# Moving four of the eight token-operand chunks to other start bytes in SBUF

## The chip, the core and the metric

The kernel runs on one NeuronCore of a Trainium2 chip. The metric is the device time of one execution in microseconds (us), the median of several runs. TensorE (PE) does the matrix products; VectorE (DVE), ScalarE (ACT) and GpSimd (POOL) do the rest; SP issues most DMAs. Every step below between two matmuls is from the start of one to the start of the next, because matmuls overlap and the duration of one is longer than the step.

## The reference

Two transformer blocks in a row on 256 tokens of width 1024. The first adds 16 meta tokens (272 rows in all), and does pooling, forgetting attention and stick-breaking attention, then a SwiGLU MLP of width 2816. The second does a gated convolution and block attention, a squared-ReLU MLP of width 4096, a linear recurrence, and a second such MLP. Cut to what carries the work:

```
proj = rmsnorm(h, norm1) @ w_in            # 1024 -> 2560 (and 6 forget logits)
h = h + concat(pool, fox, sb) @ w_out      # 1024 -> 1024
h = h + (silu(a @ w_gate) * (a @ w_up)) @ w_down          # a = rmsnorm(h, norm2), 1024 -> 2816 -> 1024
h = h + concat(conv, moba) @ ab_w_out      # from rmsnorm(h) @ ab_w_in
h = h + square(relu(rmsnorm(h) @ w_up)) @ w_down          # 1024 -> 4096 -> 1024
h = h + (rg_lru(...) * gelu(gate)) @ c_w_out
h = h + square(relu(rmsnorm(h) @ w_up)) @ w_down
out = rmsnorm(h, final_norm)
```

## The kernel before

The kernel is written out by hand for the five engines, with semaphores; every engine's order of work is the order of its code. All tokens (272 or 256 columns) stay in SBUF, with the model width on the partitions in KC = 8 chunks of 128. The weights come from HBM as 280 "slabs" of 128 x 1024 fp32, through a ring of R = 4 slots. ACT rounds each slab to fp32r (`whi`), and DVE subtracts to get the rest (`wlo`). The token operand is split in the same way into `ahi` and `alo`, so that one fp32 product is three fp32r matmuls: hi x hi, hi x lo, lo x hi. The helper `three` (L1402 to L1407) issues them.

There are two kinds of slab. A column slab (`column`, L1412) makes 128 output features: for k = 0..7 three matmuls, each with another 128 x 128 weight and with chunk k of `ahi` or `alo` as the moving operand, 24 in all. A row slab (`row`, L1462) adds to the residual: 24 matmuls that all have one moving chunk, which in the MLPs is a chunk of `hidhi` and `hidlo` (`hidden_row`, `last_rows`) and in the three output projections OUT1, OUT2 and OUT3 a chunk of `ahi` and `alo` (`operand_row`; for OUT3 chunks 0 and 1 are in `hidhi`). The MLP loops run columns and rows in turn: MLP1 has 44 columns and 22 rows, MLP2 and MLP3 32 of each; IN1, IN2 and IN3 have 20, 20 and 16 columns. After an MLP, the next stage's two first columns are issued chunk by chunk (`first_high`, `first_low`) as the operand becomes ready: ACT writes `ahi` (L563, L644, L594), DVE writes `alo` (L979, L973).

`ahi` and `alo` hold chunk k at STRIDE_A * k = 320 * k floats, which is 1280 bytes or five blocks of 256 bytes. PAD_A puts the start of both on a multiple of 256. A matmul on 256 tokens begins at token NMETA = 16, 64 bytes on; so each of the eight chunks begins at byte 64 of a block of 256. `hidhi` and `hidlo` also begin at byte 64 of a block, and each of their chunks is 1024 bytes. Matmuls on all 272 tokens (most of IN1) begin at byte 0 of a block. The weights of every matmul (`whi`, `wlo`, 512 bytes each) begin at byte 128 of a block. These places follow from the sizes of the buffers.

Of the kernel before, what the change touches and what calls it, by code (L numbers as in the profile page):

```python
# [25 lines left out]
F32 = mybir.dt.float32  # L26
F32R = mybir.dt.float32r
ALU = mybir.AluOpType
ACT = mybir.ActivationFunctionType
AX = mybir.AxisListType.X  # L30

P = 128
DM = 1024
KC = DM // P
SEQ = 256
NMETA = 16
T1 = NMETA + SEQ

STRIDE_A, PAD_A = 320, 32
EPS = 1e-6  # L40
BIG = 1.0e30

# [145 lines left out]
def build(nc, slabs, xT, par_in, fbias_in, poolw_in, gatew_in, convw_in, out):  # L188
    with ExitStack() as ctx:
        def sb(name, shape, dt=F32):  # L190
            return ctx.enter_context(nc.sbuf_tensor(name, shape, dt))
# [25 lines left out]
        whi = sb("whi", [P, R, KC, P], F32R)  # L217
        wlo = sb("wlo", [P, R, KC, P], F32R)
        h = sb("h", [P, KC, T1])
        af = sb("af", [P, KC, SEQ])  # L220

        sb("pad_a", [P, PAD_A])
        ahi = sb("ahi", [P, KC, STRIDE_A], F32R)
        alo = sb("alo", [P, KC, STRIDE_A], F32R)
        sq = sb("sq", [P, KC, T1])
        gg, half_gb = sb("gg", [P, KC]), sb("half_gb", [P, 2 * CONV_C])
        std = sb("std", [P, T1])
# [118 lines left out]
        sbs_bank = (half(gemm_bank[0], 0), half(gemm_bank[0], 1), half(aux_bank, 1))  # L346
        consts_done = 13

        def hid_buf(f, last):
            return 2 if f == last else f % 2  # L350

        def row_operand(s, k):

            if s == A_LRU and k < 2:
                return hidhi[:, k, :], hidlo[:, k, :]
            return ahi[:, k, NMETA:T1], alo[:, k, NMETA:T1]

        block = ctx.enter_context(nc.Block())

# [156 lines left out]
        def _(act):  # L516
# [40 lines left out]
            def residual_hi(i, lo=NMETA):  # L557

                for k in range(KC):
                    act.wait_ge(h_ready, KC * (i - 1) + k + 1)  # L560
                    if i < N_FINAL:
                        g = GAIN[i] + k
                        act.activation(ahi[:, k, lo:T1], h[:, k, lo:], ACT.Copy, scale=par[:, g:g + 1]).then_inc(ahi_ready, 1)  # L563
                        for j in (SQUARES_CHUNKS if i in (N_MIX0, N_MIXC) else SQUARES_ROWS).get(k, ()):
                            residual_squares(i, j)
                    else:
                        act.activation(sq[:, k, lo:], h[:, k, lo:], ACT.Square).then_inc(sq_ready, 1)  # L567
# [72 lines left out]
            for i in range(PIECES):  # L640
                act.wait_ge(x_loaded[i], 16)
                for k in (2 * i, 2 * i + 1):
                    g = GAIN[N_NORM1] + k
                    act.activation(ahi[:, k, 0:T1], h[:, k, :], ACT.Copy, scale=par[:, g:g + 1]).then_inc(ahi_ready, 1)  # L644
                for b in range(2):
                    act.wait_ge(piece_loaded[b][i], 16)
                    act.activation(whi[:, b, 2 * i:2 * i + 2, :], raw[:, b, 2 * i:2 * i + 2, :], ACT.Copy)\
                       .then_inc(hi_done if i == PIECES - 1 else piece_hi, 1)
# [294 lines left out]
        def _(dve):  # L943
# [31 lines left out]
            def residual_lo(i, s, k, lo=NMETA):  # L975

                g = GAIN[i] + k
                dve.wait_ge(ahi_ready, KC * s + k + 1)
                dve.scalar_tensor_tensor(alo[:, k, lo:T1], h[:, k, lo:], par[:, g:g + 1], ahi[:, k, lo:T1].bitcast(F32),  # L979
                                         ALU.mult, ALU.subtract).then_inc(alo_ready, 1)  # L980

            def acc_add(m, n, i, s):
# [418 lines left out]
        def _(pe):  # L1401
            def three(dst, n, j, xh, xl, start=False, stop=False):  # L1402

                hi, lo = whi[:, n % R, j, :], wlo[:, n % R, j, :]
                pe.matmul(dst, hi, xh, start=start, stop=False, skip_group_check=True)  # L1405
                pe.matmul(dst, hi, xl, start=False, stop=False, skip_group_check=True)  # L1406
                return pe.matmul(dst, lo, xh, start=False, stop=stop, skip_group_check=True)  # L1407
# [4 lines left out]
            def column(n, bank, q=0, lo=NMETA, amid=None):  # L1412

                slab_ready(n, q)
                for k in range(KC):
                    if amid and k == 3:
                        amid()
                    ins = three(bank[:, lo:T1], n, k, ahi[:, k, lo:T1], alo[:, k, lo:T1], k == 0, k == KC - 1)
                ins.then_inc(slab_used, 1)

            def first_high(n, s, k, lo=NMETA):

                pe.wait_ge(ahi_ready, KC * s + k + 1)
                for b in range(2):
                    dst, slot = gemm_bank[b][:, lo:T1], (n + b) % R
                    for w in (whi, wlo):
                        pe.matmul(dst, w[:, slot, k, :], ahi[:, k, lo:T1], start=(k == 0 and w is whi), stop=False,  # L1427
                                  skip_group_check=True)

            def first_low(n, s, k, lo=NMETA):  # L1430

                pe.wait_ge(alo_ready, KC * s + k + 1)
                for b in range(2):
                    dst, slot = gemm_bank[b][:, lo:T1], (n + b) % R
                    ins = pe.matmul(dst, whi[:, slot, k, :], alo[:, k, lo:T1], start=False, stop=(k == KC - 1),  # L1435
                                    skip_group_check=True)
                    if k == KC - 1:
                        ins.then_inc(slab_used, 1)
# [528 lines left out]
```

## Time and profile before

| | us |
|---|---|
| median of 3 runs | 877.65 (877.24, 877.65, 883.81) |
| the profiled execution | 884.41 |
| its span, first to last instruction | 882.7 |
| PE busy in it | 870.2 (99%) |
| DVE, ACT, POOL busy | 607.3, 469.2, 91.7 |
| mean granted TensorE clock | 0.998 of 2.4 GHz |

The profiled execution is 6.8 us longer than the median and 1.7 us longer than its own span. The times of the runs lie in two places, two at 877 and two (with the profiled one) at 884. Time in a part of the kernel is read from the starts of its matmuls, not from the busy time, which reads 99% at any pace.

### The profile page before, as it was taken

The page shows a single profiled execution, that of the slowest core. Times are in us where ns is not written, and L with a number is a line of the kernel's source. Part 1 is how long each engine was busy: PE and PEld are TensorE (multiplying, and loading weights), DVE is VectorE, ACT ScalarE, POOL GpSimd, SP SyncE. Part 2 cuts the span into 40 slices and gives each one's busy share as a digit, 9 for nine tenths or more (in the row PEclk, how much of TensorE's full clock was granted, in tenths as well). Part 3 has the DMA queues.
Part 4 walks back from the last instruction along what each step waited for, and adds up shares of the span by engine and source line. Part 5 has one row for each costly group of instructions (what it writes and reads, how often), then busy time and mean ns, then how long its engine had stood idle before and what let it go on. Part 6 is the DMA issues. An engine that isn't in the chain of part 4 may idle for free.

```text
span 882.7 us, 19329 instructions
## 1 busy us (share of the span) xinstructions
PE 870.2 (99%) x7298; PEld 837.3 (95%) x7298; DVE 607.3 (69%) x997; ACT 469.2 (53%) x754; POOL 91.7 (10%) x147
## 2 busy tenths in 40 slices
PE   9999999999999999999999999999999999999997
PEld 8988899999999999788999999999998999999996
DVE  5776567656656587778866666668979966666665
ACT  5646766443444485448644444445786644444443
POOL 4220001000000039520100000002110100000001
PEclk9999999999999999999999999999999999999999
DMA  7532247655565557525465555554444565555551
GB/s 254 166 120 96 97 143 250 187 183 191 173 205 173 187 161 235 163 97 178 140 212 186 185 180 182 189 191 144 171 141 168 168 212 185 181 185 187 186 171 48
DMA packets 44290, 151.61 MB, mean 172 GB/s; under 512 B 5588, under 2 KB 6868, under 8 KB 44244
## 3 DMA queue, kind: packets, MB, share of 16 engines
q1 hardware_dynamic: 41040, 145.00, 50.1%
q0 software_dynamic: 2400, 4.89, 1.7%
q10 hardware_dynamic: 804, 1.06, 0.3%
q8 instruction: 33, 0.54, 0.3%
q14 instruction: 13, 0.11, 0.0%
HBM read 148.14 MB, written 1.05 MB: 169 GB/s over the span
## 4 chain that ended last, share of the span: by engine, by line
PE 87%; DVE 6%; ACT 3%; issue 1%; DMA 1%; POOL 1%; SPq 0%; DVEq 0%; ACTq 0%; POOLq 0%
PE bank L1405 26%; PE bank L1407 26%; PE bank L1406 26%; DVE alo L979 2%; PE bank L1799 1%; DVE wlo L955 1%; PE bank L1435 1%; PE bank L1571 1%; DVE h L989 1%; PE bank L1548 1%; PE bank L1427 1%; PE bank L1889 1%; PE bank L1519 1%; DMA raw<-in_slabs 1%; ACT whi L535 1%
## 5 line engine op out<-in xcount | busy, mean ns | idle before, releaser
L1405 PE MATMUL bank<-ahi,whi 128*128 128x256 f32 (+1 forms) x1392 | 398.1, 286 | 1.0 <-DVE alo L973 0.7
L1406 PE MATMUL bank<-alo,whi 128*128 128x256 f32 (+1 forms) x1392 | 391.0, 281 | 0.0
L1407 PE MATMUL bank<-ahi,wlo 128*128 128x256 f32 (+1 forms) x1392 | 390.9, 281 | 0.0
L955 DVE TENSOR_TENSOR wlo<-raw,whi 128x1024 fp32r<-128x1024 f32 x272 | 331.0, 1225 | 26.6 <-ACT whi L535 26.6
L535 ACT ACTIVATE whi<-raw 128x1024 fp32r<-128x1024 f32 x272 | 281.2, 1050 | 92.4 <-PE bank L1407 82.7
L1405 PEld LDWEIGHTS bank<-ahi,whi 128*128 128x128 f32 x1392 | 263.0, 189 | 5.8 <-DVE alo L973 2.3
L1406 PEld LDWEIGHTS bank<-alo,whi 128*128 128x128 f32 x1392 | 264.2, 190 | 0.4
L1407 PEld LDWEIGHTS bank<-ahi,wlo 128*128 128x128 f32 x1392 | 261.5, 188 | 0.0
L1405 PE MATMUL bank<-hidhi,whi 128*128 128x256 f32 x704 | 197.8, 281 | 0.6 <-DVE wlo L955 0.6
L1406 PE MATMUL bank<-hidlo,whi 128*128 128x256 f32 x704 | 197.7, 281 | 0.0
L1407 PE MATMUL bank<-hidhi,wlo 128*128 128x256 f32 x704 | 197.7, 281 | 0.0
L1406 PEld LDWEIGHTS bank<-hidlo,whi 128*128 128x128 f32 x704 | 134.0, 190 | 0.0
L1405 PEld LDWEIGHTS bank<-hidhi,whi 128*128 128x128 f32 x704 | 133.2, 189 | 0.8 <-issue 0.8
L1407 PEld LDWEIGHTS bank<-hidhi,wlo 128*128 128x128 f32 x704 | 132.2, 188 | 0.0
L1287 DVE SCALAR_TENSOR_TENSOR y<-bank,rstd 128x256 f32<-128x256 f32 x64 | 27.1, 424 | 123.7 <-PE bank L1407 121.7
L860 ACT ACTIVATE hidhi<-y 128x256 fp32r<-128x256 f32 x64 | 26.8, 419 | 132.6 <-DVE y L1287 129.4
L403 POOL TENSOR_TENSOR sq<-sq 128x256 f32<-128x256 f32 (+1 forms) x19 | 16.2, 865 | 319.7 <-ACT sq L567 176.3
L408 POOL TENSOR_TENSOR sq<-sq 128x256 f32<-128x256 f32 x12 | 9.6, 804 | 359.4 <-ACT sq L553 181.1
L998 DVE SCALAR_TENSOR_TENSOR proj<-bank,rstd 128x256 f32<-128x256 f32 (+1 forms) x56 | 23.5, 424 | 33.0 <-PE bank L1407 30.2
L746 ACT ACTIVATE hidhi<-y 128x256 fp32r<-128x256 f32 x22 | 9.2, 418 | 59.0 <-DVE y L1171 59.0
L979 DVE SCALAR_TENSOR_TENSOR alo<-h,par,ahi 128x256 fp32r<-128x256 f32 (+1 forms) x48 | 29.2, 671 | 0.0
L1295 DVE TENSOR_TENSOR hidlo<-y,hidhi 128x256 fp32r<-128x256 f32 x64 | 27.2, 425 | 2.3
(236 smaller groups left out, 724.7 us busy)
## 6 DMA issues: line engine op xcount, KB each, us to landing
raw<-in_slabs SPq DMA_DIRECT2D x272, 512.0 KB, 3.5
shared<-in_convw POOLq DMA_DIRECT2D x4, 512.0 KB, 6.8
shared<-zpad POOLq DMA_DIRECT2D x48, 35.5 KB, 3.5
raw<-in_slabs SPq DMA_DIRECT2D x8, 128.0 KB, 5.9
vtok<-in_gatew POOLq DMA_DIRECT2D x2, 512.0 KB, 4.8
out<-y SPq DMA_DIRECT2D x4, 256.0 KB, 2.3
h<-in_xT ACTq DMA_DIRECT2D x3, 272.0 KB, 5.9
h<-in_xT SPq DMA_DIRECT2D x1, 272.0 KB, 3.3
```

What stands on the lines that cost most here:

```text
L403: pool.tensor_tensor(a, a, sq[:, 2 * j + 1, lo:], ALU.add).then_inc(sum_ready, 1)
L408: ins = pool.tensor_tensor(sq[:, a, NMETA:], sq[:, a, NMETA:], sq[:, b, NMETA:], ALU.add)
L535: act.activation(whi[:, n % R, :, :], raw[:, n % R, :, :], ACT.Copy).then_inc(hi_done, 1)
L860: act.activation(hidhi[:, hid_buf(f, FF2 - 1), :], hid[:, f % 2, :], ACT.Square).then_inc(hid_hi, 1)
L955: dve.tensor_tensor(wlo[:, n % R, :, :], raw[:, n % R, :, :], whi[:, n % R, :, :].bitcast(F32), ALU.subtract).then_inc(lo_done, 1)
L979: dve.scalar_tensor_tensor(alo[:, k, lo:T1], h[:, k, lo:], par[:, g:g + 1], ahi[:, k, lo:T1].bitcast(F32), ALU.mult, ALU.subtract).then_in ...
L998: dve.scalar_tensor_tensor(proj[:, d, lo:], src[:, lo:T1], scale, rstd[:, lo:], ALU.mult, ALU.mult).then_inc(gemm_evac, 1)
L1287: dve.scalar_tensor_tensor(hid[:, f % 2, :], col_bank(f)[:, NMETA:T1], 0.0, rstd[:, NMETA:], ALU.max, ALU.mult).then_inc(gemm_evac, 1)
L1295: dve.tensor_tensor(hidlo[:, b, :], hid2[:, f % 2, :], hidhi[:, b, :].bitcast(F32), ALU.subtract).then_inc(hid_lo, 1)
L1405: pe.matmul(dst, hi, xh, start=start, stop=False, skip_group_check=True)
L1406: pe.matmul(dst, hi, xl, start=False, stop=False, skip_group_check=True)
L1407: return pe.matmul(dst, lo, xh, start=False, stop=stop, skip_group_check=True)
```

## The change

Three of the last four chunks of `ahi` and `alo` begin later in their 1280 bytes: chunk 4 by 32 floats (128 bytes), chunk 5 by 48 (192 bytes), chunk 7 by 16 (64 bytes). With the 64 bytes of the meta tokens, chunks 4 to 7 begin at bytes 192, 0, 64 and 128 of a block of 256; chunks 0 to 3 still at 64. On all 272 tokens the starts of chunks 4 to 7 are at 128, 192, 0 and 64, those of chunks 0 to 3 at 0. Every reader and writer goes through the new helper `chunk`. The buffers have the same sizes, so nothing else moves in SBUF. No instruction is added, removed or moved, and every shape and wait stays.

```diff
+SHIFTED = {4: 32, 5: 48, 7: 16}
...
-        ahi = sb("ahi", [P, KC, STRIDE_A], F32R)
-        alo = sb("alo", [P, KC, STRIDE_A], F32R)
+        ahi = sb("ahi", [P, KC * STRIDE_A], F32R)
+        alo = sb("alo", [P, KC * STRIDE_A], F32R)
...
+        def chunk(buf, k, lo=0):
+            c = STRIDE_A * k + SHIFTED.get(k, 0)
+            return buf[:, c + lo:c + T1]
...
-            return ahi[:, k, NMETA:T1], alo[:, k, NMETA:T1]
+            return chunk(ahi, k, NMETA), chunk(alo, k, NMETA)
...
-                        act.activation(ahi[:, k, lo:T1], h[:, k, lo:], ACT.Copy, scale=par[:, g:g + 1]).then_inc(ahi_ready, 1)
+                        act.activation(chunk(ahi, k, lo), h[:, k, lo:], ACT.Copy, scale=par[:, g:g + 1]).then_inc(ahi_ready, 1)
...
-                dve.scalar_tensor_tensor(alo[:, k, lo:T1], h[:, k, lo:], par[:, g:g + 1], ahi[:, k, lo:T1].bitcast(F32),
+                dve.scalar_tensor_tensor(chunk(alo, k, lo), h[:, k, lo:], par[:, g:g + 1], chunk(ahi, k, lo).bitcast(F32),
...
-                    ins = three(bank[:, lo:T1], n, k, ahi[:, k, lo:T1], alo[:, k, lo:T1], k == 0, k == KC - 1)
+                    ins = three(bank[:, lo:T1], n, k, chunk(ahi, k, lo), chunk(alo, k, lo), k == 0, k == KC - 1)
```

`first_high`, `first_low` and the first stage's write of `ahi` are changed in the same way.

## Rows read from the trace of the kernel before

**Rows 1.** The page, parts 1 and 4: busy time, and the chain that ended last
```profile
PE 870.2 (99%) x7298; PEld 837.3 (95%) x7298; DVE 607.3 (69%) x997; ACT 469.2 (53%) x754; POOL 91.7 (10%) x147
...
PE 87%; DVE 6%; ACT 3%; issue 1%; DMA 1%; POOL 1%; SPq 0%; DVEq 0%; ACTq 0%; POOLq 0%
```
**Rows 2.** Stretches inside MLP1, MLP2, MLP3, then late in IN3: busy, count, clock
```profile
143.76:316.19 172.43, 172.43 (x1467) 172.43 (x1466) 108.74 (x149) 78.06 (x105) 0.00 (x0) 1.00 0.62 195
438.28:607.88 169.60, 169.60 (x1443) 169.60 (x1441) 106.93 (x157) 74.16 (x92) 0.00 (x0) 1.00 0.57 189
701.50:868.27 166.77, 166.77 (x1419) 166.77 (x1417) 104.37 (x153) 72.17 (x90) 0.00 (x0) 1.00 0.54 178
650.91:659.38 8.47, 8.32 (x74) 8.12 (x72) 6.42 (x13) 8.43 (x13) 0.00 (x0) 1.00 0.27 89
```
**Rows 3.** Timeline of PE in MLP1, a column and then a row
```profile
143.52 0.28 PE L1406 MATMUL bank<-alo,whi 128*128 128x256 f32 x1
143.64 0.28 PE L1407 MATMUL bank<-ahi,wlo 128*128 128x256 f32 x1
143.76 0.28 PE L1405 MATMUL bank<-hidhi,whi 128*128 128x256 f32 x1
...
144.47 0.28 PE L1405 MATMUL bank<-hidhi,whi 128*128 128x256 f32 x1
```
**Rows 4.** Timeline of PE at the end of IN3: column, then a row of OUT3
```profile
665.05 0.28 PE L1405 MATMUL bank<-ahi,whi 128*128 128x256 f32 x1
...
665.39 0.28 PE L1405 MATMUL bank<-hidhi,whi 128*128 128x256 f32 x1
...
666.07 0.28 PE L1405 MATMUL bank<-hidhi,whi 128*128 128x256 f32 x1
```
**Rows 5.** Groups of matmuls by shape over the whole span: busy us, mean ns
```profile
L1406 PE MATMUL bank<-alo,whi 128*128 128x256 f32 x1288 | 360.9, 280 | 0.0
...
L1406 PE MATMUL bank<-hidlo,whi 128*128 128x256 f32 x704 | 197.7, 281 | 0.0
```
**Rows 6.** The same view, of a stretch late in IN3
```profile
L1406 PE MATMUL bank<-alo,whi 128*128 128x256 f32 x25 | 6.9, 276 | 0.0
```
**Rows 7.** Timeline of PE: two columns of IN3 and IN2 after a stall
```profile
647.98 0.47 PE L1405 MATMUL bank<-ahi,whi 128*128 128x256 f32 x1
648.29 0.28 PE L1406 MATMUL bank<-alo,whi 128*128 128x256 f32 x1
648.41 0.28 PE L1407 MATMUL bank<-ahi,wlo 128*128 128x256 f32 x1
648.52 0.28 PE L1405 MATMUL bank<-ahi,whi 128*128 128x256 f32 x1
648.64 0.28 PE L1406 MATMUL bank<-alo,whi 128*128 128x256 f32 x1
648.75 0.28 PE L1407 MATMUL bank<-ahi,wlo 128*128 128x256 f32 x1
648.87 0.28 PE L1405 MATMUL bank<-ahi,whi 128*128 128x256 f32 x1
648.98 0.28 PE L1406 MATMUL bank<-alo,whi 128*128 128x256 f32 x1
...
335.83 0.47 PE L1405 MATMUL bank<-ahi,whi 128*128 128x256 f32 x1
336.13 0.28 PE L1406 MATMUL bank<-alo,whi 128*128 128x256 f32 x1
...
336.96 0.28 PE L1407 MATMUL bank<-ahi,wlo 128*128 128x256 f32 x1
```
**Rows 8.** Timeline of PE in IN1: 272 columns from byte 0, then 256 from byte 64
```profile
28.30 0.29 PE L1407 MATMUL bank<-ahi,wlo 128*128 128x272 f32 x1
...
29.44 0.29 PE L1407 MATMUL bank<-ahi,wlo 128*128 128x272 f32 x1
29.57 0.28 PE L1405 MATMUL bank<-ahi,whi 128*128 128x256 f32 x1
29.68 0.28 PE L1406 MATMUL bank<-alo,whi 128*128 128x256 f32 x1
...
30.25 0.28 PE L1405 MATMUL bank<-ahi,whi 128*128 128x256 f32 x1
```
**Rows 9.** Writers of the operand: timeline of DVE, then ACT's and DVE's durations
```profile
425.97 2.74 DVE L989 TENSOR_TENSOR h<-bank,h 128x256 f32<-128x256 f32 x8
...
L979 DVE SCALAR_TENSOR_TENSOR alo<-h,par,ahi x48: 471/495/1046, 8.3 to 695.6; 128x256 fp32r<-128x256 f32 x40, 128x272 fp32r<-128x272 f32 x8
...
L563 ACT ACTIVATE ahi<-h,par x40: 492/495/511, 128.9 to 693.5; 128x256 fp32r<-128x256 f32 x40
```

More of the change, by code:

```diff
@@ L643, in _ @@
                     g = GAIN[N_NORM1] + k
-                    act.activation(ahi[:, k, 0:T1], h[:, k, :], ACT.Copy, scale=par[:, g:g + 1]).then_inc(ahi_ready, 1)
+                    act.activation(chunk(ahi, k), h[:, k, :], ACT.Copy, scale=par[:, g:g + 1]).then_inc(ahi_ready, 1)
                 for b in range(2):
@@ L1426, in first_high @@
                     for w in (whi, wlo):
-                        pe.matmul(dst, w[:, slot, k, :], ahi[:, k, lo:T1], start=(k == 0 and w is whi), stop=False,
+                        pe.matmul(dst, w[:, slot, k, :], chunk(ahi, k, lo), start=(k == 0 and w is whi), stop=False,
                                   skip_group_check=True)
@@ L1434, in first_low @@
                     dst, slot = gemm_bank[b][:, lo:T1], (n + b) % R
-                    ins = pe.matmul(dst, whi[:, slot, k, :], alo[:, k, lo:T1], start=False, stop=(k == KC - 1),
+                    ins = pe.matmul(dst, whi[:, slot, k, :], chunk(alo, k, lo), start=False, stop=(k == KC - 1),
                                     skip_group_check=True)
```

## The prediction

> **What bounds the kernel now.** I read the page first: PE is busy 99% of the span, and 87% of the chain that ended last is PE [rows 1]. So the time is the number of matmuls times their step, plus the hand-overs between stages. The change touches neither the count, nor an order, nor a wait. What it can touch is the step, so I read starts, in the timeline and in the windows.
>
> In the MLPs, which hold 194 of the 280 slabs, the step is the same everywhere. In MLP1 the window of 172.43 us has 1467 matmul records, about three of them begun before it, so 1464: 117.8 ns each. MLP2 and MLP3 give the same: 169.60 us over 1440, 166.77 us over 1416 [rows 2]. The timeline shows it singly: 143.76 to 144.47 is six steps in 0.71 us, 118 ns, and it doesn't change where a column (moving operand `ahi`) hands over to a row (`hidhi`) [rows 3].
>
> The same instructions on the same addresses also run faster. At the end of IN3 the steps are 0.34 us for three and 0.68 us for six, 113.3 ns, again across the hand-over from column to row [rows 4]. The clock is 1.00 (the level of 2.4 GHz) at both places [rows 2], so it isn't the clock. There are thus **two steady paces, 117.8 and 113.3 ns**, 4.44 ns apart, and the operand's start byte (64 for all of them) doesn't alone decide between them. The duration that the page gives tells them apart too: 281 ns in the slow pace. The 704 of `hidlo` read 281 on average, so nearly all of them are slow; the 1288 of `alo` read 280.2 (360.9 us / 1288) [rows 5]. In the fast pace one reads 276 [rows 6], in a stretch of IN3 that has 74 records in 8.47 us with its stalls [rows 2]. So about 16% of the `ahi` and `alo` matmuls are fast, some 620 of 3864.
>
> What picks the pace? After a stall of PE a column can go either way. At 648.29 the steps are 120, 110, 120, 110, 120 ns in rounded figures and then 113; five steps take 0.58 us where five fast ones take 0.567, so the settling cost 13 ns. At 336.13 the seven steps to 336.96 take 0.83 us, 118.6 ns each, and it stays slow [rows 7]. Without a stall neither pace leaves its rut: MLP1 keeps one step for 172 us. The one place where the start byte changes with no stall is in IN1, from 272 columns at byte 0 to 256 at byte 64. Nine steps before it take 1.14 us (126.7 each); behind it six steps take 0.68 us, 113.3 at once [rows 8].
>
> The runs agree: 877.2 and 877.7 against 883.8 and the profiled 884.4, 6.8 us apart. One of the MLPs 2 and 3 is 64 slabs x 24 = 1536 matmuls, and 1536 x 4.44 ns = 6.8 us. I read this as one MLP that fell into the fast pace in two of the four executions. In the profiled one all three are slow.
>
> **The change, part by part.** The writers cost nothing. DVE's and ACT's instructions keep their shapes. DVE's eight adds to `h`, whose chunks are 1088 bytes apart and so begin at four different bytes of a block, take 2.74 us together, 0.34 each, with no pause; L979 and L563 have minima and medians within 24 and 3 ns of each other [rows 9], although they read those same chunks of `h`. If this cover failed, it would be 40 instructions by perhaps 24 ns, 1 us.
>
> The readers carry everything. Each column now has five changes of start byte with no stall: 64 to 192, to 0, to 64, to 128, and back to 64. That makes 164 columns x 5 = 820 changes in the kernel, where before there were hardly any. An `operand_row` of chunk 4, 5 or 7 has 24 matmuls at another byte, nine rows in all.
>
> What a change of byte does is in no row but one, the change in IN1, and there the fast pace came at once. So my step is: the slow pace depends on each matmul being like the last, a change of the start byte inside every column breaks it, and the fast pace survives. The gain if all goes fast:
> - The three MLP stretches: 1464 + 1440 + 1416 = 4320 matmuls x 4.44 ns = 19.2 us.
> - The rest of the MLPs: 194 x 24 = 4656, less 4320, is 336 x 4.44 = 1.5 us.
> - Outside the MLPs: 3864 less 108 MLP columns x 24 = 2592 leaves 1272, of which 620 are fast, so 650 x 4.44 = 2.9 us. Many of these lie behind real stalls, where the first steps are long in either pace [rows 7]; I take half, 1.4 us.
>
> Together 22.1 us. Against it stands what a change costs: from nothing (the row of IN1 [rows 8]) to a settling as behind a stall, 13 ns at 648.29 [rows 7]; with rounding up to 20. Over 820 changes that is 0 to 16 us. The nearest row is the one without a stall, so I stay near the lower end and take one change in four at 19 ns, 3.8 us. The sum: 884.41 - 22.1 + 3.8 = **866.1 us** (860.4 if a change costs nothing and the last 1.9 us come too, 878 at the dear end). The sum stands against the profiled execution, which is 6.8 us over the median; against 877.65 it is -1.3%. That the bar is the median takes away a third of the gain: part of it is had by luck already.
>
> The Trainium skill speaks against any effect. In "SBUF — State Buffer", section "Who interferes with whom", PE has a read port for the moving operand and one for the weights, independent of each other, and never waits on anyone; no page ties a matmul's speed to its start byte. By that rule the step stays what it was, and the time with it. The trace does not contradict it outright, but it shows two paces for one instruction, which the rule leaves no room for.
>
> **The rivals.**
>
> *Slower: the slow pace survives and the new bytes are dearer.* Byte 0 is the only other start that a long stretch shows: 272 columns at 126.7 ns [rows 8]. At the granted 2.4 GHz the 16 extra columns are 6.7 ns, which leaves 120.0 ns for 256, 2.2 above the slow pace; and no stretch of 272 was seen in a faster pace. If chunks 4, 5 and 7 all step so, it is 164 columns x 9 x 2.2 = 3.3 us. If in addition the fast pace is the one that doesn't survive the changes, the 620 fast matmuls lose 620 x 4.44 = 2.8 us. From the profiled execution's 884.4 that gives 887.7 to 890.5. It decides from where a change throws PE out of the fast pace more often than out of the slow one. For it: in 508 us of MLP the slow pace never broke [rows 2], though columns and rows alternate there; the fast stretches are short. Against it: the row of IN1, and the runs at 877, in which a fast MLP seems to have held for about 170 us.
>
> *Half: the fixed parts go fast, the shifted ones don't.* In a column, chunks 4 to 7 and 0 (15 matmuls) are held at about 117.8 by the changes, and 9 run at 113.3; rows run fast. 86 MLP rows x 24 x 4.44 = 9.2 us and 108 x 9 x 4.44 = 4.3 us gained, and some 26 fast columns outside lose 26 x 15 x 4.44 = 1.7 us: 884.4 - 11.8 = 872.6 us.
>
> *The change does nothing:* what picks the pace is the phase at the last stall, as now, and every run draws it per stage. Then the median stays where it was, 877.65, between 877 and 884.4. For it: both paces exist at one and the same set of addresses [rows 3, 4]. This is also what the page cited above would give.
>
> **How the numbers follow.** Forecast 0.45, of which 0.41 lies below 868.9; slower 0.26; nothing 0.17; half 0.12. A measurement of this kernel can tell about 1% from no change, so the bounds are 868.9 and 886.4 us. Faster: 0.41 and 0.01 of the half case, 0.42. Slower: 0.26 and 0.01 of the case in which nothing happens, 0.27. Within 1%: 0.31. The range runs from 858 (all fast, and a little gained at a byte that suits better than 64) to 891 (the dear end of the slower case); it leaves out about one case in ten above and one in twenty below. The likeliest case alone runs from 860 to 871. The range is wide, since the price of a change of byte rests on one row and the sign hangs on it.
>
> **What would show each step.** In the timeline inside an MLP, the step in rows (`hidhi`) should be 113.3 and the page should read 276 ns for them instead of 281. Within a column, the steps of matmuls 13 to 24 and of the next slab's first three show the price of a change; chunk 5 at 120 ns would speak for the slower case. The windows of MLP1, MLP2 and MLP3 should be about 7.0, 6.8 and 6.8 us shorter, less the changes. L979 and L563 should keep 495 ns. Repeated runs should no longer lie in two places 6.8 us apart. The prediction is wrong if rows still step at 117.8: then the start byte doesn't break the slow pace. It is wrong in size if rows step at 113.3 but columns take more than 2.76 us.

## The result and the profile after

| | before, us | after, us |
|---|---|---|
| median of 22 runs each | 883.29 (870.45 to 884.11) | 871.82 (870.92 to 873.03) |
| the profiled execution | 884.41 | 870.92 |
| its span | 882.7 | 869.2 |
| PE, DVE, ACT busy | 870.2, 607.3, 469.2 | 857.8, 607.5, 469.5 |
| mean granted clock | 0.998 | 0.999 |

The ratio is 0.9905 [0.9883, 0.9926]. It leaves out the runs of a kernel that are more than 1.5% above its fastest one, which for before means those above 883.5 us, though by their times they are of one kind with its runs at 882.7 to 883.5; the ratio of the two medians is 0.987.

More runs of before show what three could not. Over all comparisons in this study it ran 72 times: 8 times at 869.7 to 871.1 us, 31 times at 876.2 to 878.0, 33 times at 882.4 to 884.7, and never in between. The medians of the three places, 870.7, 877.0 and 883.4, are 6.3 and 6.4 us apart, about what one MLP in the fast pace is worth by the prediction (6.8 us), so I read them as two, one or none of its three MLPs in the fast pace. No trace shows before itself at 870 or 877.

How often each place comes differs between the five sets of runs that the 72 are made of: in the set above 16 of 22 lie at 882.7 to 884.1, in the set beside `only_chunk4` none of 13 (median 876.9), in the set beside `all_240` 4 of 17 (median 877.2). The sets beside the experiments ran on four different chips; whether the chip decides this is not shown. So the median of 877.65 that the prediction was given is one of the two that before shows, neither rare nor safe.

The changed kernel has one place in its 22 runs, 2.1 us wide. So the change removes a lottery. It wins 11.5 us against before's median in the same set and 13.5 us between the profiled executions; against a median of 877 it would win some 5 us, and against before's best place (median 870.7) it loses 1.1 us.

**Windows.** Stretches inside MLP1, MLP2 and MLP3 of after (columns of numbers as in [rows 2]):
```profile
142.76:314.40 171.64, 171.64 (x1490) 171.64 (x1489) 110.65 (x153) 80.56 (x112) 0.69 (x1) 1.00 0.62 200
436.70:599.30 162.60, 162.60 (x1418) 162.60 (x1417) 104.16 (x152) 72.87 (x90) 0.00 (x0) 1.00 0.59 194
695.11:855.00 159.89, 159.89 (x1395) 159.89 (x1394) 101.71 (x148) 70.82 (x88) 0.00 (x0) 1.00 0.55 183
```
With three records taken off, as in the prediction, 171.64 us over 1487 steps is 115.4 ns; the two others give 114.9. Before it was 117.8 in all three [rows 2]. The clock is 1.00 in both, the level of 2.4 GHz. The step is neither of the two paces, so it is a mixture, and the timeline has to say of what.

**Timeline.** PE in MLP1 of after, one column behind a row (chunk 0 from 153.86, chunks 4, 5, 6, 7 from 155.22, 155.57, 155.93, 156.28), then the start of the next column:
```profile
153.86 0.28 PE L1411 MATMUL bank<-ahi,whi 128*128 128x256 f32 x1
...
155.22 0.28 PE L1411 MATMUL bank<-ahi,whi 128*128 128x256 f32 x1
...
155.57 0.28 PE L1411 MATMUL bank<-ahi,whi 128*128 128x256 f32 x1
...
155.93 0.28 PE L1411 MATMUL bank<-ahi,whi 128*128 128x256 f32 x1
...
156.28 0.28 PE L1411 MATMUL bank<-ahi,whi 128*128 128x256 f32 x1
...
156.63 0.29 PE L1411 MATMUL bank<-ahi,whi 128*128 128x256 f32 x1
```
Chunks 0 to 3 take 1.36 us for 12 steps, 113.3 ns. Chunks 4 to 7 take 1.41 us for their 12, 117.5 in these rounded figures. Singly, by starts to 1 ns and within 1 ns from column to column, chunk 4 steps 118, 118, 117, chunk 5 118, 119, 117, chunk 6, which stands at byte 64 like the fixed ones, 117, 117, 117, and chunk 7 120, 118, 117. The next slab then begins with 121, 121, 116, 114 and is at 113.3 from there. That pattern repeats in every column of the three MLPs' loops. A slab of 24 matmuls takes 2.774 us as a column behind a row, 2.793 as a column behind a column and 2.739 as a row; before, each of them took 2.827 (24 x 117.8), and in the fast pace throughout it would be 2.720.

**The balance.** 86 rows win 0.088 us each, 7.6 us. Of the columns, 22 stand behind a column and win 0.034, 86 behind a row and win 0.053: 5.3 us. Together 12.9 of the 13.5 us between the two profiled executions.

**Where the slow pace ends.** Late in IN3 two columns begin in the slow pace, behind a stall at 638.93. PE of after, the first of them from its second matmul, then the starts of the two next columns:
```profile
639.24 0.28 PE L1412 MATMUL bank<-alo,whi 128*128 128x256 f32 x1
...
641.95 0.28 PE L1411 MATMUL bank<-ahi,whi 128*128 128x256 f32 x1
...
644.78 0.29 PE L1411 MATMUL bank<-ahi,whi 128*128 128x256 f32 x1
...
645.25 0.28 PE L1412 MATMUL bank<-alo,whi 128*128 128x256 f32 x1
...
645.93 0.28 PE L1412 MATMUL bank<-alo,whi 128*128 128x256 f32 x1
```
The first takes 2.71 us for its last 23 steps and the second 2.83 for 24, 117.8 and 117.9 each: all five changes of byte in the first, the return to 64 at 641.95 included, left the pace slow. Behind the second one's chunk 7, at 644.78, the steps are 121, 122, 115, 115, and from 645.25 six take 0.68 us, 113.3 each.

In six columns outside the MLPs the slow pace ends earlier, ahead of any chunk 7. One of them, PE in IN2, the starts of chunks 1, 4, 6 and 7:
```profile
379.52 0.28 PE L1411 MATMUL bank<-ahi,whi 128*128 128x256 f32 x1
...
380.58 0.28 PE L1411 MATMUL bank<-ahi,whi 128*128 128x256 f32 x1
...
381.29 0.28 PE L1411 MATMUL bank<-ahi,whi 128*128 128x256 f32 x1
...
381.63 0.28 PE L1411 MATMUL bank<-ahi,whi 128*128 128x256 f32 x1
```
Chunks 1 to 3 are in the slow pace (nine steps in 1.06 us, 117.8), and chunk 6, back at byte 64 behind chunks 4 and 5, steps at 113.3 (three in 0.34 us).

**Groups.** By shape over the whole span of after:
```profile
L1412 PE MATMUL bank<-alo,whi 128*128 128x256 f32 x1288 | 359.0, 279 | 0.0
...
L1412 PE MATMUL bank<-hidlo,whi 128*128 128x256 f32 x704 | 194.8, 277 | 0.0
```
The `hidlo` group fell from 281 to 277 ns, nearly the 276 of the fast pace [rows 5, 6], the `alo` group from 280 to 279 only. The writer that the prediction asked about did not move (DVE's shortest, median and longest in ns; [rows 9] had 471/495/1046):
```profile
L985 DVE SCALAR_TENSOR_TENSOR alo<-h,par,ahi x48: 469/492/974, 7.2 to 686.5; 128x256 fp32r<-128x256 f32 x40, 128x272 fp32r<-128x272 f32 x8
```

**New bytes on their own.** OUT3's rows of chunks 5 and 7 are 24 matmuls at one byte each. PE of after, first chunk 5 (byte 0), then chunk 7 (byte 128):
```profile
672.80 0.28 PE L1411 MATMUL bank<-ahi,whi 128*128 128x256 f32 x1
...
673.40 0.28 PE L1413 MATMUL bank<-ahi,wlo 128*128 128x256 f32 x1
...
678.78 0.28 PE L1411 MATMUL bank<-ahi,whi 128*128 128x256 f32 x1
...
679.38 0.28 PE L1413 MATMUL bank<-ahi,wlo 128*128 128x256 f32 x1
```
At byte 128 five steps take 0.60 us, 120.0 ns each. At byte 0 the steps run 120, 119, 115, 117, 122 and again, 118.7 on average. The rows of chunk 4 (byte 192) step at 117.8. None of them has the pace of 113.3.

### The profile page after: what moved, and what is told of

It reads as the page before. It is cut to its first block, busy times and chain, and to the rows that moved or that the text cites. A ratio compares the mean times of both kernels' runs of the same rounds, so it can differ in the third digit from the quotient of the medians.

```text
span 869.2 us, 19329 instructions
## 1 busy us (share of the span) xinstructions
PE 857.8 (99%) x7298; PEld 825.1 (95%) x7298; DVE 607.5 (70%) x997; ACT 469.5 (54%) x754; POOL 94.1 (11%) x147
## 3 DMA queue, kind: packets, MB, share of 16 engines
q10 hardware_dynamic: 804, 1.06, 0.4%
## 4 chain that ended last, share of the span: by engine, by line
PE 88%; DVE 6%; ACT 3%; issue 1%; POOL 1%; DMA 1%; SPq 0%; DVEq 0%; ACTq 0%; POOLq 0%
PE bank L1411 26%; PE bank L1413 26%; PE bank L1412 26%; DVE alo L985 2%; PE bank L1805 1%; DVE wlo L961 1%; PE bank L1441 1%; PE bank L1433 1%; PE bank L1577 1%; PE bank L1554 1%; PE bank L1895 1%; PE bank L1525 1%; DVE h L995 1%; ACT whi L541 1%; DVE t L1344 1%
## 5 line engine op out<-in xcount | busy, mean ns | idle before, releaser
L1411 PE MATMUL bank<-hidhi,whi 128*128 128x256 f32 x704 | 195.3, 277 | 0.5 <-DVE wlo L961 0.5
L1412 PE MATMUL bank<-hidlo,whi 128*128 128x256 f32 x704 | 194.8, 277 | 0.0
L1413 PE MATMUL bank<-hidhi,wlo 128*128 128x256 f32 x704 | 194.6, 276 | 0.0
```

## The experiments

The theory after the result, K below: byte 64 has two paces, each keeps itself, and which one it is gets drawn anew at an irregularity. The return from byte 128 to 64 behind chunk 7 is such a "kick" and ends in the fast pace; chunks 4 and 5 only cost. (The last point holds for chunk 4, which was run alone. Chunk 5 was not, and the column at 379.52 above speaks against it.) Its rivals were that each change of byte does a part, that the mean over many bytes is what is faster, and later that any disturbance or any extra work would do. Unless said otherwise, a kernel is the changed one with the edit shown.

### 1. Chunk 7 alone (`only_chunk7`)
```diff
-SHIFTED = {4: 32, 5: 48, 7: 16}
+SHIFTED = {7: 16}
```


> Only chunk 7 of ahi and alo is moved, to byte 128; chunks 0 to 6 stay at 64. Theory K (kick): the gain comes from leaving and coming back to byte 64, once per column; the matmuls at other bytes are themselves slow. Then rows step at 113.3 ns, columns too but for three matmuls at about 120 and four that settle: a column behind a row 2.74 us, behind a column 2.76, a row 2.74, and the time is 866 us (871.8 less 164 columns x 0.034). Rival R (rotation): several different bytes in a row are needed, or the change at chunk 4 is the one that helps: then rows and chunks 0 to 6 stay at 117.8 and the time is 883 or above, as before.

Measured: 866.13 us (865.54 to 866.99, 4 runs), ratio 0.9842 [0.9786, 0.9899]. Window of MLP2:
```profile
434.64:590.00 155.36, 155.36 (x1368) 155.36 (x1367) 99.44 (x144) 70.53 (x87) 0.00 (x0) 1.00 0.60 196
```
155.36 us over 1365 is 113.8 ns. A column ends with three steps of 119, 113, 116 and the next slab begins with 122, 116, 114; all else is at 113.3. So one shifted chunk brings the whole gain, and chunks 4 and 5 take 5.7 us of it back. The return from chunk 7 doesn't end the slow pace each time. In IN2 and in IN3 two columns in a row are at 117.8 behind a stall (329.47 to 335.31 and 635.37 to 641.22): the return behind the first changes nothing, as at 641.95 of after, and the one behind the second turns it fast. Once fast, a run of columns and rows stays so.

### 2. One matmul of a column (`only_lo_chunk7`)
Only `alo` of chunk 7 stands at byte 128: one matmul in 24.
```diff
-SHIFTED = {4: 32, 5: 48, 7: 16}
+SHIFTED = {}
+SHIFTED_LO = {7: 16}
...
-            c = STRIDE_A * k + SHIFTED.get(k, 0)
+            c = STRIDE_A * k + (SHIFTED_LO if buf is alo else SHIFTED).get(k, 0)
```


> Only chunk 7 of alo is at byte 128, one matmul in 24 of a column; ahi is as before. Theory K: one matmul at another byte is a kick too. Then a column costs 23 steps of 113.3, one of 120 and a settling of 19 ns: 2.745 us, rows 2.72 to 2.74, the time 863 to 866 us. Rival: one matmul is too short to leave the slow pace, or throws PE out of the fast one: rows stay at 117.8 and the time is 880 to 885.

Measured: 866.61, 872.39, 872.65, 866.35 us, ratio 0.989 [0.9823, 0.9957]. In the profiled execution (866.61), behind a stall, MLP1's first row and two columns ran at 117.8; the row behind them began 117, 117, 123, 118 and was at 113.3 from its fifth step. The window in MLP2:
```profile
435.07:590.00 154.93, 154.93 (x1363) 154.93 (x1362) 98.79 (x143) 70.33 (x87) 0.00 (x0) 1.00 0.59 196
```
That is 113.9 ns. So one matmul at another byte can end the slow pace, but does not each time: the first of these two columns had one as well and stayed slow. Two of four runs are 6 us longer, the size of one MLP at 117.8. Where those two spent it no trace shows.

### 3. Finer bytes (`fine_bytes`)
Chunks 0 to 7 at bytes 64, 80, 96, 112, 144, 160, 224, 240, to read each from its rows in OUT1, OUT2 and OUT3.
```diff
-SHIFTED = {4: 32, 5: 48, 7: 16}
+SHIFTED = {1: 4, 2: 8, 3: 12, 4: 20, 5: 24, 6: 40, 7: 44}
```


> Chunks 0 to 7 begin at bytes 64, 80, 96, 112, 144, 160, 224 and 240 of a block of 256. The rows of OUT1, OUT2 and OUT3 have 24 matmuls each at one byte and show its steady step. Theory K says nothing of single bytes; if the step goes by 64-byte units, 80 to 112 give the paces of 64 (113.3 or 117.8) or one unit more, 144 and 160 that of 128 (120.0), 224 and 240 that of 192 (117.8). If finer, each byte has its own step. Time 865 to 885 us.

Measured: 877.59 us (one run). The step of the rows' 24 matmuls once it has settled: byte 80 about 119, 96 about 118.6, 112 about 117, 144 113.3 in two rows of three, 160 117 to 118, 224 about 120, 240 113.3 in all three. PE in the row of chunk 7, byte 240, in OUT2:
```profile
423.16 0.28 PE L1411 MATMUL bank<-ahi,whi 128*128 128x256 f32 x1
...
423.50 0.28 PE L1411 MATMUL bank<-ahi,whi 128*128 128x256 f32 x1
...
424.52 0.28 PE L1411 MATMUL bank<-ahi,whi 128*128 128x256 f32 x1
```
Nine steps from 423.50 take 1.02 us, 113.3 ns. The step thus changes with shifts as small as 16 bytes. That chunks lie on different bytes is no gain in itself: this kernel's columns take 2.827 to 2.857 us, no better than before.

### 4. Weights at byte 192 (`weights_at_192`)
All moving operands as before (byte 64); 64 bytes of padding ahead of the weight buffers move `whi` and `wlo` from byte 128 to 192.
```diff
-SHIFTED = {4: 32, 5: 48, 7: 16}
...
+        sb("pad_w", [P, 16])
...
-        sb("pad_a", [P, PAD_A])
+        sb("pad_a", [P, PAD_A - 16])
```


> The kernel before with a pad of 64 bytes ahead of the weight slabs, so that all weights begin at byte 192 in place of 128; ahi, alo and hidhi stay at byte 64. Theory P (pair): the step goes by the start of the moving operand against that of the weights, as if two reads met. Moving 64 with weights 192 is the distance of moving 0 with weights 128, whose step in the changed kernel is 118.7 ns; so the MLPs step at 118.7, the time is 888 us, and no second pace is seen. Rival M (moving operand alone): the steps stay 117.8 or 113.3, the time 870 to 884 us.

Measured: 889.85 us (one run). A window in MLP2, and PE in a row of MLP1:
```profile
443.79:600.00 156.21, 156.21 (x1319) 156.21 (x1318) 95.68 (x139) 68.00 (x84) 0.00 (x0) 1.00 0.57 188
```
```profile
152.25 0.28 PE L1406 MATMUL bank<-hidhi,whi 128*128 128x256 f32 x1
...
152.84 0.28 PE L1408 MATMUL bank<-hidhi,wlo 128*128 128x256 f32 x1
```
156.21 us over 1316 is 118.7 ns; the five steps of the timeline take 0.59 us, and singly they repeat 120, 119, 115, 117, 122, those of byte 0 in after. Moving 64 against weights 192 is as far apart as moving 0 against weights 128. So the moving operand's own byte does not decide alone: where the weights begin counts too, and the simplest reading is that the **distance from the weights' start** is what counts. One pair of places at one distance carries this reading, with one run; other distances were not tried with moved weights.

### 5. Everything at one other byte (`all_240`, `all_144`)
Before's layout, with the padding ahead of `ahi` made longer. It was meant to put all moving operands, `hidhi` and `hidlo` too, at byte 240 and 144.
```diff
-        sb("pad_a", [P, PAD_A])
+        sb("pad_a", [P, PAD_A + 44])
```
(`PAD_A + 20` for the other.)

> The kernel before with 176 bytes more of padding ahead of ahi, so that all eight chunks and hidhi and hidlo begin at byte 240 (on all 272 tokens at 176); no chunk is shifted against another. Theory P2: what counts is the distance from the start of the weights (byte 128), and at 240 there is only the fast pace, as in the three output rows of the run with fine bytes. Then every stall ends in 113.3 ns, the MLPs step at it from their start, and the time is 860 us (883.5 less some 5400 slow matmuls x 4.44 ns), the same in each run. Rival: the three rows went fast by chance, and byte 240 has a slow pace too; then the times lie in several places between 862 and 884 us.

> The same with 80 bytes more, so that all operands begin at byte 144. Theory P2: at 144 two of three output rows of the run with fine bytes went to 113.3 ns and one to a step of about 118.5, so there are two paces, and the runs lie in several places between 860 and 886 us. Rival: like 240, one pace, 860 us.

Measured: 889.59 us (889.25 to 891.85, 6 runs), ratio 1.0171 [1.0132, 1.0211]; and 880.57 (878.85 to 883.07, 10 runs), ratio 1.0058 [1.0032, 1.0084]. MLP2 of the first, then of the second:
```profile
443.70:600.00 156.30, 156.30 (x1320) 156.30 (x1319) 95.71 (x140) 68.00 (x84) 0.00 (x0) 1.00 0.57 187
```
```profile
440.00:600.00 160.00, 160.00 (x1374) 160.00 (x1373) 99.52 (x146) 70.46 (x87) 0.00 (x0) 1.00 0.57 190
```
They give 118.7 and 116.7 ns. Neither tested what it was made for. The buffers' places afterwards showed that a buffer's size is rounded up to 32 bytes, so the operands began at bytes 0 and 160. Read at their true bytes they fit: byte 0 everywhere is 118.7 with the same single steps as in experiment 4, and 160 is the 117 to 118 of `fine_bytes`. Byte 160 has more than one pace too: in MLP3 of the second kernel a slab takes 2.83 us, in MLP1 and MLP2 2.80. They also show that a kernel with all operands on one byte can lie 5 us above the slowest of before's 72 runs.

### 6. All chunks at byte 192 (`all_192`)
```diff
-SHIFTED = {4: 32, 5: 48, 7: 16}
+SHIFTED = {k: 32 for k in range(8)}
```


> All eight chunks of ahi and alo at byte 192, hidhi and hidlo still at 64. In the changed kernel and in three output rows the step at 192 was 117.8 ns, never 113.3. If byte 192 has the slow pace alone, all columns step at 117.8 (2.827 us) and the time is 878 to 885 us, with rows at 64 in either pace. If the step has a period of 128 bytes in the distance from the weights, 192 is like 64 and has the fast pace too: then some columns of 2.72 us are seen, most of all in the stages with many stalls (IN1, IN2, IN3).

Measured: 881.12 us (one run). Columns (192) and MLP rows (`hidhi`, still 64) now alternate. PE in MLP2, end of a row, then a column:
```profile
448.98 0.28 PE L1411 MATMUL bank<-hidhi,whi 128*128 128x256 f32 x1
...
449.32 0.28 PE L1411 MATMUL bank<-ahi,whi 128*128 128x256 f32 x1
...
450.03 0.28 PE L1411 MATMUL bank<-ahi,whi 128*128 128x256 f32 x1
```
Here the row steps at 113.3 (three in 0.34 us) and the column behind it at 118 (six steps in 0.71 us). In MLP1 and MLP3, though, the rows stayed at 117.6, with the same two bytes taking turns. So a change between 64 and 192 does not break the slow pace at 64, and in MLP2 the fast one survives it. Byte 192 itself stepped at 113.3 in five slabs, each behind a stall, so it has two paces too. One of them, PE in IN2:
```profile
383.81 0.28 PE L1411 MATMUL bank<-ahi,whi 128*128 128x256 f32 x1
...
385.51 0.28 PE L1411 MATMUL bank<-ahi,whi 128*128 128x256 f32 x1
```
That is fifteen steps in 1.70 us, 113.3 each. Behind another, at the end of IN3, the fast pace did not survive the change from 192 to 64: from 662.12 on the rows step at 117 to 119.

### 7. A kick with no operand moved (`kick_once`)
Before's layout; three redundant matmuls of 128 columns ahead of the first row of each MLP, into a bank that the row then starts afresh.
```diff
+            def kick():
+                for _ in range(3):
+                    pe.matmul(acc_bank[0][:, 0:P], ones_r[:, :], ones_r[:, :], start=True, stop=True,
+                              skip_group_check=True)
...
+            kick()
             hidden_row(0, MLP1 + 4, 0, first=True)
...
+                kick()
                 hidden_row(0, base + 3, m0, first=True)
```


> The kernel before with three extra matmuls of 128 columns (ones_r by ones_r, into a bank that the next matmul overwrites) ahead of the first row of each of the three MLPs; nothing else. Theory K: the pace is drawn anew at each irregularity and then kept. Then in each MLP the step can differ before and behind the extra matmuls, and behind them it stays one and the same to the MLP's end; the time is 884.3 less 6.8 us for each MLP that turns fast: 863.5, 870, 877 or 884. Rival R: the fast pace needs a change in every column to be kept; then one event changes nothing and all MLPs step at 117.8, 883 to 884 us.

Measured: 864.50 us (863.94 to 865.48, 4 runs), ratio 0.9884 [0.9833, 0.9935]. PE around the kick in MLP1, and a window in MLP2:
```profile
142.34 0.28 PE L1405 MATMUL bank<-ahi,whi 128*128 128x256 f32 x1
...
142.57 0.28 PE L1407 MATMUL bank<-ahi,wlo 128*128 128x256 f32 x1
142.69 0.45 PE L1491 MATMUL bank<-ones_r 128*128 128x128 f32 x3
142.97 0.33 PE L1405 MATMUL bank<-hidhi,whi 128*128 128x256 f32 x1
143.15 0.28 PE L1406 MATMUL bank<-hidlo,whi 128*128 128x256 f32 x1
...
143.60 0.28 PE L1407 MATMUL bank<-hidhi,wlo 128*128 128x256 f32 x1
```
```profile
433.50:590.00 156.50, 156.50 (x1383) 156.50 (x1382) 100.30 (x146) 71.33 (x89) 0.00 (x0) 1.00 0.60 196
```
Ahead of the kick the steps are 118 (142.34 to 142.69 is three in 0.35), behind it 113 (143.15 to 143.60 is four in 0.45), and every later slab of that MLP takes 2.720 us. Nine added matmuls do all the work of the shift and leave no price in the columns. This shows two things: the gain is the pace at byte 64, and a pace once entered is kept for 170 us.

It does not show what in the three matmuls is the kick. `ones_r` is moving operand and weight at once, and by the buffers' places it begins at byte 64 (512 bytes of `tri_r` behind the 8192 of `hidhi` and `hidlo`). Its matmuls thus stand at distance 0 from their weights, as chunk 7 at byte 128 does from weights at 128, and not at the distance of all others. They also have 128 columns, a weight of their own, and follow each other at other steps. No run separates these.

### 8. Extra work of the usual form (`same_matmuls`)
The control to 7: at the same places three redundant matmuls `whi` x `hidhi`, 256 columns from byte 64.
```diff
+            def same(n, m):
+                pe.wait_ge(hid_lo, m + 1)
+                slab_ready(n)
+                for _ in range(3):
+                    pe.matmul(acc_bank[0][:, 0:SEQ], whi[:, n % R, 0, :], hidhi[:, 0, :], start=True, stop=True,
+                              skip_group_check=True)
```


> A control for kick_once: at the same three places three extra matmuls, but of the form of all others (256 columns from hidhi at byte 64, a weight of the slab), so that nothing is irregular. Theory K: the extra matmuls keep the pace in which PE is; MLPs step at 117.8 behind them as before them, and the runs lie where those of the kernel before lie, plus 1.1 us for nine matmuls: 871, 878 or 884.5 us. Rival: any extra work or pause at that place turns the MLPs fast; then 865 to 866 us each time.

Measured: 878.25 us (10 runs, six at 877.35 to 878.36, four at 883.91 to 884.78), ratio 1.002 [0.9966, 1.0073]. MLP1, then MLP2 of the profiled execution (877.76):
```profile
148.86:300.00 151.14, 151.14 (x1336) 151.14 (x1335) 96.24 (x131) 67.64 (x94) 0.00 (x0) 1.00 0.61 196
440.00:600.00 160.00, 160.00 (x1361) 160.00 (x1360) 99.39 (x145) 69.48 (x86) 0.00 (x0) 1.00 0.55 187
```
113.4 and 117.8 ns. The times stay in two of before's places, and MLP2 stayed slow behind them, so extra work does not set the pace each time. MLP1 did turn fast at these very matmuls: they use one weight three times running, which also breaks the order hi, lo, hi. So they may be a weaker kick rather than none: by the times one MLP went fast in six of ten runs here (how many of these at the extra matmuls no trace shows), and all three in each of the four runs of `kick_once`. This is moreover the trace of an execution at 878 us: one MLP is fast and two are slow.

### 9. A kick at another moment (`kick_early`)
`kick()` not ahead of the first row but right behind the statistics of MLP1, IN2, MLP2, IN3 and MLP3, where PE has just waited.

> The kernel before with the three short matmuls right behind the statistics of MLP1, IN2, MLP2, IN3 and MLP3, at the start of each stage's unbroken stretch, in place of ahead of the first row. Theory K: the two or three columns between go fast too, 3 x 2 x 0.107 = 0.6 us, and IN2's nine columns 1 us: 862 to 864 us. Rival: which pace a kick gives depends on the phase at which it comes, and behind the statistics (fp32 matmuls) it comes at another phase than in kick_once: some stages stay at 117.8, and the time is 866 to 884 us.

Measured: 872.20, 865.51, 865.20, 870.46 us, ratio 0.9872 [0.9753, 0.9991]. MLP1, then MLP2 of the profiled execution (872.20):
```profile
149.87:300.00 150.13, 150.13 (x1277) 150.13 (x1276) 91.97 (x126) 65.42 (x90) 0.00 (x0) 1.00 0.59 189
441.00:590.00 149.00, 149.00 (x1317) 149.00 (x1316) 95.35 (x138) 67.76 (x84) 0.00 (x0) 1.00 0.58 197
```
MLP1 stayed at 117.8, with its kick, while MLP2 and MLP3 went at 113.4. PE around the kick of MLP1:
```profile
138.04 0.63 PE L1491 MATMUL bank<-ones_r 128*128 128x128 f32 x3
138.51 0.33 PE L1405 MATMUL bank<-ahi,whi 128*128 128x256 f32 x1
138.68 0.28 PE L1406 MATMUL bank<-alo,whi 128*128 128x256 f32 x1
...
139.27 0.28 PE L1405 MATMUL bank<-ahi,whi 128*128 128x256 f32 x1
```
The kick is followed by an unbroken run of matmuls, and these step at 118 at once (five in 0.59 us). So a kick is a new draw, not a cure, and a wait behind it isn't what spoils it. What differs from `kick_once` is what comes ahead: there the kick broke into a run of matmuls in the slow pace, here it comes behind the fp32 matmuls of the statistics, where in the same execution it came out fast for MLP2 and MLP3. Which of this matters is open. The theory's 862 to 864 us was missed by all four runs; the slow MLP1 is what the rival said.

### 10. Chunk 4 alone (`only_chunk4`)
```diff
-SHIFTED = {4: 32, 5: 48, 7: 16}
+SHIFTED = {4: 32}
```


> Only chunk 4 of ahi and alo is moved, to byte 192; the rest at 64. In the run all_192 whole columns at 192 stepped at 117.8 ns and in MLP1 and MLP3 the rows at 64 kept that step, so a change between 64 and 192 need not end the slow pace. Theory: the shift of chunk 4 is a cost of the change and not its gain; the columns step at 117.8 in chunk 4 always, the slow pace can outlive it, and the time is 874 to 885 us, above that of chunk 7 alone (866.1). Rival R: any change of byte in each column ends the slow pace; then rows step at 113.3, and the time is 865 to 868 us.

Measured: 877.76 us (871.55 to 883.58, 10 runs, in three places), ratio 1.0018 [0.9988, 1.0047]. MLP2 of the profiled execution (883.44):
```profile
440.47:600.00 159.53, 159.53 (x1357) 159.53 (x1356) 98.05 (x142) 69.63 (x87) 0.00 (x0) 1.00 0.60 190
```
117.8 ns, and the lottery is back. Two changes of byte in each column, to 192 and back, did not end the slow pace. Not every change of byte is a kick. No run has chunk 5 (byte 0) alone. Since chunk 4 alone did not end the slow pace here, the six columns of after that are fast in chunk 6 point at byte 0 as a second kick; that is argued and not shown.

### 11. Everything truly at byte 240 (`true_240`)
```diff
-SHIFTED = {4: 32, 5: 48, 7: 16}
+SHIFTED = {k: 44 for k in range(8)}
...
-        hidhi = sb("hidhi", [P, 4, SEQ], F32R)
-        hidlo = sb("hidlo", [P, 4, SEQ], F32R)
+        hidhi = sb("hidhi", [P, 4 * SEQ + 64], F32R)[:, 44:44 + 4 * SEQ].rearrange("p (a b) -> p a b", a=4)
+        hidlo = sb("hidlo", [P, 4 * SEQ + 64], F32R)[:, 44:44 + 4 * SEQ].rearrange("p (a b) -> p a b", a=4)
```


> All chunks of ahi and alo, and of hidhi and hidlo, really begin at byte 240, by offsets inside their buffers (the pad of the run all_240 was rounded up, which put its operands at byte 0). Theory P2: at 240 there is only the fast pace (three of three output rows of the run with fine bytes). Then all stages step at 113.3 ns from every stall on, and the time is 859 to 862 us in each run. Rival: 240 has slow paces too, which single rows missed by luck; then MLPs in the profile step at 116 to 120 ns and the runs lie at 866 to 890 us.

Measured: 863.53 us (862.95 to 863.92, 4 runs), ratio 0.9833 [0.972, 0.9947], the lowest median of the study, though 1 to 2 us above what was expected. A window in MLP2, and PE behind the stall at MLP2's start:
```profile
433.19:590.00 156.81, 156.81 (x1386) 156.81 (x1385) 101.08 (x147) 71.74 (x89) 0.00 (x0) 1.00 0.57 197
```
```profile
427.83 0.28 PE L1412 MATMUL bank<-alo,whi 128*128 128x256 f32 x1
...
429.00 0.28 PE L1413 MATMUL bank<-ahi,wlo 128*128 128x256 f32 x1
429.11 0.28 PE L1411 MATMUL bank<-ahi,whi 128*128 128x256 f32 x1
```
From 427.83 to 429.00 there are ten steps in 1.17 us, 117 each, and the next is 0.11; the window gives 113.4. At this distance from the weights the slow steps are only passed through, about ten of them behind each stall. Behind every stall of the profiled execution the matmuls of 256 columns came to 113.3, in all stages, and the four runs lie within 1 us.

## Why the prediction was right in kind and wrong in size

- **Two paces, 4.44 ns apart, at one clock:** right. `kick_once` shows both within one MLP, 1 us apart, and its time is 0.7% below even before's best place.
- **What the three runs meant:** the reading (one MLP fast per 6.8 us) holds; `same_matmuls`, a kernel with nine matmuls more, shows it in a trace at 877.76. But four executions showed two of three places: there is a third at 870, and how often each comes differs from set to set.
- **Writers cost nothing:** right.
- **A change of byte breaks the slow pace and the fast one survives:** right for the kernel, too general as a step. Of its five changes per column the two at chunk 7, to byte 128 and back, are enough (`only_chunk7`), though they may take a second column; those at chunks 4 and 5 ended the slow pace too, in six columns. The change to 192 and back does not (`only_chunk4`, `all_192`).
- **Rows at 113.3, MLP windows shorter:** the rows take 2.739 us rather than 2.720, since each pays the return from a chunk 7.
- **The price of the changes, 3.8 us: this is the term that failed.** Of the 22.1 us, 13.5 came, so the price was 8.6 us, 10.5 ns for each of 820 changes where I took 3.8 us, 4.6 ns each (one in four at 19). It lay inside the bounds that I gave (0 and 16 us), but the value within them was a choice, and what I had mis-seen is what the price consists of. I priced it as a settling *at* the change, by a row of IN1 in which fast came at once. The traces show that the settling is there, 19 ns, but only once per column, in the next slab's first four steps. The larger part is the bytes' own step: twelve matmuls per column that take 1413 ns, by the single steps above, in place of 1360: 53 ns. That sum, 72 ns a column, over the 108 MLP columns is 7.8 us.
- **The rivals.** *Half* came true, at 872.6 forecast against 871.82 and 870.92: fixed parts and rows fast, shifted ones slow. I gave it 0.12. That it is so near is in part luck: it had 15 slow matmuls in a column where there are 12, and nothing for a settling that costs 19 ns. *Slower* named the right fact, that byte 0 is dearer (118.7 measured, 120.0 estimated from a row of 272 columns), and that byte 128 costs 120.0; it missed that the slow pace at byte 64 would go. *The change does nothing* is refuted: rows step at 113.3, and 22 runs lie within 2.1 us, where before's spread over 14.
- **What should have led to Half:** the profile showed no stretch of byte 0 in a faster pace, and the prediction says so. I used that for the slow case alone and not to price the shifted chunks in my own.
- **Slips in the sums, under 1 us together:** the cheap end should add the 1.5 us left outside the MLPs and not 1.9 (860.8, not 860.4); 205 changes at 19 ns are 3.9 us; and [rows 5] leave out the two first columns of each stage, so that 3864 less 102 MLP columns x 24 leaves 1416 matmuls outside the MLPs, not 1272.

The rule against any effect, from the Trainium skill, "SBUF — State Buffer", section "Who interferes with whom", was that PE has a port for each operand and never waits on anyone. The runs contradict what I drew from it: the step goes from 113.3 to 120.0 ns by where the moving operand starts, and moving the weights alone put a run 5 us above the slowest of before's 72 (889.85 against 884.67).

**Which version to use.** `true_240` 863.5, `kick_once` 864.5, `only_chunk7` 866.1, the change as made 871.8. Each of the first three kept one place in four runs. The first and the third rest on the layout alone; `kick_once` hangs on the moment of the kick (`kick_early`).

**What stays open:** which mechanism inside the chip keeps the two paces; what makes three matmuls a kick, and why its moment matters; whether chunk 5 alone would do it; whether the distance is what counts at other places than the one pair tried; and whether the 272-column matmuls of IN1 (126.7 ns) have a better place. No run here settles these.

## What to carry to other kernels

Read the step from start to start of back-to-back matmuls, and compare the same instruction at different times: a busy share of 99% hides 4% of pace. If a kernel's runs lie in a few places at equal distances, suspect a draw at a stall that then persists, run it twenty times rather than three, and look for a layout in which only one pace exists before pricing a change by one row. When a padding is to place an operand, read the address that came out, since the allocator may round it.

## What the runs showed of the hardware that I had not expected

- An fp32r matmul of 256 columns steps at 113.3, 116.7, 117.8, 118.7 or 120.0 ns at a granted 2.4 GHz, depending on where its moving operand and its weights start (bytes 64, 160 and 192 against weights at 128 showed more than one pace each), with shifts as small as 16 bytes. The Trainium skill, "TensorE: Matmul & The Clock Gate", section "Wait — 56ns, not 53.3ns?", has N / 2.4 GHz + about 2.5 ns, from which I estimate 109.2 ns; no steady stretch of these matmuls in any trace here was below 113.
- At one and the same set of addresses two paces can hold, each for 170 us, and nine matmuls of 128 columns in the whole kernel decide 6 to 20 us (864.5 against before's 870.7 to 884.4).
- A buffer's size in SBUF was rounded up to 32 bytes: paddings of 304 and 208 bytes took 320 and 224 (`all_240`, `all_144`).
